# Stores ahead of the waits at stage ends, gathers in their own stage, and another order of loads and spreading units in a streaming encoder step

## The reference, cut to what matters

```python
a = rmsnorm(h, lw['norm_mix'])
z = a @ lw['w_in']                    # q, k, v, gates of both mixers
y_m, C, n, m = mlstm_chunkwise(...)   # 4 heads of 256, state C, n, m
y_f = fox_block(...)                  # 16 heads of 64, forgetting attention; sample tokens also see a cache
merge = jax.nn.sigmoid(gm) * (y_m @ lw['w_br_m']) + jax.nn.sigmoid(gf) * (y_f @ lw['w_br_f'])
h = h + merge @ lw['w_out']
h = h + peer(rmsnorm(h, lw['norm_ffn']), lw['peer_w_q'], lw['peer_keys1'], lw['peer_keys2'], lw['peer_u'], lw['peer_v'])
h = h + jax.nn.sigmoid(e @ lw['w_ple_gate']) * (p @ lw['w_ple_proj'])   # e = rmsnorm(h, lw['norm_ple'])
```

## Time and profile before

| | |
|---|---|
| median of 3 runs | 4817.5 us (4817.3 to 4831.1) |
| profiled execution | 4826.2 us, its span 4824.5 us |
| TensorE (PE) busy | 4326.6 us, 90% of the span |
| VectorE (DVE) busy | 2995.7 us, 62% |
| ScalarE (ACT) busy | 999.4 us, 21% |
| GpSimd (POOL) busy | 1260.4 us, 26% |
| bytes moved | 1477.7 MB, mean 306 GB/s |

### The profile page before, as it was taken

One profiled execution on the slowest core, in us unless ns is written; L12 is line 12 of the kernel. 1 busy time (PEld: TensorE's weight loads), 2 busy tenths in 40 slices (PEclk: granted clock), 3 DMA queues, 4 the chain that ended last, 5 costly groups with the idle time before them and its releaser, 6 DMA issues. The chain is left out here.

```text
span 4824.5 us, 49007 instructions
## 1 busy us (share of the span) xinstructions
PE 4326.6 (90%) x16974; PEld 2667.5 (55%) x16974; DVE 2995.7 (62%) x6257; ACT 999.4 (21%) x1991; POOL 1260.4 (26%) x969
## 2 busy tenths in 40 slices
PE   8997686989999996888887988869999999999988
PEld 5555453665555554666664666654545454544534
DVE  1002241458777767888870587767888777777733
ACT  1113321111001104555551122220000000000023
POOL 0000031014444442333320000004444444444400
PEclk9998788999999997878878999989999999999999
DMA  4443496769999998988958777749999999999941
GB/s 169 143 147 98 146 320 265 284 236 421 385 382 391 384 355 284 335 307 313 343 209 331 278 267 262 241 155 418 419 407 408 419 419 419 416 414 409 418 177 58
DMA packets 363496, 1477.74 MB, mean 306 GB/s; under 512 B 38338, under 2 KB 178418, under 8 KB 242706
## 3 DMA queue, kind: packets, MB, share of 16 engines
q0 software_dynamic: 119872, 824.76, 42.4%
q1 hardware_dynamic: 193874, 625.13, 34.9%
q10 hardware_dynamic: 49536, 25.17, 1.7%
HBM read 1369.00 MB, written 115.38 MB: 308 GB/s over the span
## 5 line engine op out<-in xcount | busy, mean ns | idle before, releaser
L2558 POOL DMA_INDIRECT ex_uv<-in_uv,idx x768 | 1169.6, 1523 | 1683.4 <-DVE ex_acc L2615 1487.8
L2599 DVE CUSTOM_DVE_ANT_0 ex_uv<-ex_uv,ex_xp 128x1024 f32<-128x1024 f32 x768 | 912.9, 1221 | 296.2 <-DMA ex_uv<-in_uv,idx 249.6
L2615 DVE SCALAR_TENSOR_TENSOR ex_acc<-ex_uv,ex_wt,ex_acc 128x1024 f32<-128x1024 f32 x768 | 943.0, 1281 | 10.3 <-DVE C L897 3.2
L392 PE MATMUL proj_psum_acc<-proj_w,aT_later 128*128 128x385 f32 x2304 | 748.7, 487 | 8.0 <-DMA proj_w<-in_w_in 8.0
L2813 PE MATMUL exp_psum_dn<-exp_dn_big,exp_dn_gg 128*128 128x512 f32 x1536 | 686.6, 597 | 28.3 <-DVE exp_dn_gg L2769 28.1
L2804 PE MATMUL exp_psum_dn<-exp_dn_xT,exp_dn_big 128*128 128x384 f32 x2048 | 684.3, 488 | 7.6 <-DMA exp_dn_big<-in_ud 7.6
L392 PEld LDWEIGHTS proj_psum_acc<-proj_w,aT_later 128*128 128x128 f32 x2304 | 437.0, 190 | 319.3 <-DMA proj_w<-in_w_in 8.2
L2804 PEld LDWEIGHTS exp_psum_dn<-exp_dn_xT,exp_dn_big 128*128 128x128 f32 x2048 | 390.5, 191 | 307.7 <-issue 71.2
L2813 PEld LDWEIGHTS exp_psum_dn<-exp_dn_big,exp_dn_gg 128*128 128x128 f32 x1536 | 291.8, 191 | 379.1 <-issue 351.5
L301 PE MATMUL proj_psum_acc<-proj_w,aT 128*128 128x385 f32 x1152 | 377.1, 488 | 4.2 <-DMA proj_w<-in_w_in 2.3
L301 PEld LDWEIGHTS proj_psum_acc<-proj_w,aT 128*128 128x128 f32 x1152 | 218.3, 190 | 158.9 <-issue 4.5
(11 more groups left out here) (460 smaller groups left out, 4237.1 us busy)
## 6 DMA issues: line engine op xcount, KB each, us to landing
proj_w<-in_w_in SPq DMA_DIRECT2D x48, 1540.0 KB, 7.7
rt_w<-in_w_q SPq DMA_DIRECT2D x36, 2048.0 KB, 8.7
exp_dn_big<-in_ud SPq DMA_DIRECT2D x128, 512.0 KB
exp_dn_big<-in_vd SPq DMA_DIRECT2D x128, 512.0 KB, 8.0
scratch_z<-proj_zs SPq DMA_DIRECT2D x216, 192.5 KB, 2.0
rt_w<-in_w_br_m SPq DMA_DIRECT2D x18, 2048.0 KB, 9.4
rt_w<-in_w_br_f SPq DMA_DIRECT2D x18, 2048.0 KB, 10.6
rt_w<-in_w_out SPq DMA_DIRECT2D x18, 2048.0 KB, 8.2
```

The source lines that it names most:

```text
L392: mm = pe.matmul(acc[j % SLOTS][:, 0:CW], aT[:, k, t * P:(t + 1) * P], w[:, u % U, k, :], start=(k == 0), stop=(k == KD - 1))
L2558: pool.indirect_dma_start(self.uv[:, slot, :], None, self.uv_tab, bass.IndirectOffsetOnAxis(ap=self.idx[:, at:at + 1], axis=0)).then_inc(s ...
L2599: dve.tensor_tensor_reduce(self.uv[:, slot, 0:D], self.uv[:, slot, 0:D], self.xp[:], 1.0, 0.0, ALU.mult, ALU.add, self.dot[:, g % 2, j:j + ...
L2615: dve.scalar_tensor_tensor(out=self.acc[:, j % 2, :], in0=self.uv[:, slot, D:2 * D], scalar=self.wt[:, g % 2, j:j + 1], in1=self.acc[:, j ...
```

## The change

It has five parts. (1) At the end of an attention stage SP issues the states, the last y, ncs and the last expert sum, and only then waits for landings. (2) The gathers of a hosted span begin in its own stage: `pool_ahead` fetches the first two groups of each span, and a span no longer fetches groups beyond its end. (3) The sample stage: n and m are loaded by ScalarE, the mLSTM's q, k, o, v go ahead of the states, half of the states go behind the next cache loads, and the y stores of the last two steps are issued by SP. (4) Spreading units: 28 in the steps 2 to 4 and 12 in the last, and named places for them; the third piece of the choice moves behind the next step's first four units. (5) The dense experts: the first two u blocks are loaded ahead of h, and their scores run ahead of the products that put h in place.

```diff
@@ FoxPrompt, MlstmPrompt, Gates
     def sp_last(self, sp):
-        self.sp_y(sp, H_F // 2 - 1)
         for s in range(2):
...
-    def sp_last(self, sp):
+    def sp_state(self, sp):
         NC = self.c1 - self.c0
...
+    def sp_last(self, sp):
+        if self.c1 == PT:
             sp.wait_ge(self.outs, (H_M + 2) * 16)
-        sp.wait_ge(self.y_out, NC * 16)
+        sp.wait_ge(self.y_out, (self.c1 - self.c0) * 16)
...
-    def sp_last(self, sp):
+    def sp_ncs(self, sp):
         if self.t0 == 0:
             sp.wait_ge(self.summed, 5)
...
@@ stage_attend
+            ml.sp_state(sp)
+            fx.sp_y(sp, H_F // 2 - 1)
+            ga.sp_ncs(sp)
+            if ex:
+                ex.store(sp, ex.nt - 1)
             fx.sp_last(sp)
             ml.sp_last(sp)
             ga.sp_last(sp)
             if ex:
-                ex.rows_end(sp, g1)
+                sp.wait_ge(ex.stored, ex.nt * 16)
@@ FoxSample.sp_first
         self.sp_k(sp, 0)
-        self.sp_v(sp, 0)
-        self.sp_k(sp, 1)
@@ MlstmSample
-    def sp_first(self, sp):
-        sp.dma_start(self.n_all[:].rearrange("p n h j -> p (n h j)"), self.T["n0"]).then_inc(self.state_in, 16)
+    def act_first(self, act):
+        act.dma_start(self.n_all[:].rearrange("p n h j -> p (n h j)"), self.T["n0"]).then_inc(self.state_in, 16)
...
-        for i in range(2):
-            self.sp_state(sp, i)
-        self.sp_load(sp, 0)
@@ stage_sample
             fx.sp_first(sp)
-            ml.sp_first(sp)
+            ml.sp_load(sp, 0)
+            ml.sp_state(sp, 0)
+            fx.sp_v(sp, 0)
+            fx.sp_k(sp, 1)
+            ml.sp_state(sp, 1)
...
             ml.sp_last(sp)
+            for s in range(STEPS - 2, STEPS):
+                fx.store_y(sp, s, y_last)
+            sp.wait_ge(ml.outs, 32)
+            sp.wait_ge(y_last, 2 * 8 * 16)
...
-            for s in range(STEPS):
-                fx.pool_y(pool, s)
+            for s in range(STEPS - 2):
+                fx.store_y(pool, s, fx.y_out[s % 2])
@@ Spread
-    PER_STEP = 24
+    PER_STEP = 28
+    PLACES = dict(y=(0, 4), b1=(4, 10), b3=(10, 16), x=(16, 18), q1=(18, 22), s=(22, 25), m=(25, 28))
+    LAST = dict(y=(0, 4), q1=(4, 8), s=(8, 12))
...
+    def at(self, i, place):
+        n = (i - self.FROM) * self.PER_STEP
+        full = n + self.PER_STEP <= self.UNITS
+        return self.units(i, *(self.PLACES if full else self.LAST).get(place, (0, 0)))
@@ stage_route, tensor: each spread(t, a, b) becomes place(t, name), as here
-                for u in spread(t, 10, 14):
+                for u in place(t, "b3"):
                     so.pe_spread(pe, u)
                 turn_x(t)
@@ stage_route, vector
+                    ones(t, 14, 18)
+                    if t >= 1:
+                        ch.piece(dve, chose, 7)
+                    ones(t, 18, 22)
+                else:
+                    ones(t, 4, 8)
+                    for n in (5, 6, 7):
+                        ch.piece(dve, chose, n)
+                    ones(t, 8, 12)
...
-                for u in spread(t, 18, 24):
-                    so.dve_one(dve, u)
                 if more:
+                    ones(t, 22, 28)
                     dve.wait_ge(s_out, (t + 1) * 4)
-                    for n in (0, 1, 2):
+                    for n in (0, 1):
                         ch.piece(dve, tiles[t], n)
                     if t >= Spread.FROM:
-                        for u in spread(t + 1, 0, 4):
-                            so.dve_one(dve, u)
+                        ones(t + 1, 0, 4)
+                    ch.piece(dve, tiles[t], 2)
@@ Experts
     def pool_ahead(self, pool, g0):
-        if g0 == 0:
-            for g in range(self.AHEAD):
-                self.fetch(pool, g)
+        for g in range(g0, g0 + self.AHEAD):
+            self.fetch(pool, g)
...
-            if g + self.AHEAD < self.GROUPS:
+            if g + self.AHEAD < g1:
                 self.fetch(pool, g + self.AHEAD)
@@ Dense
         sp.dma_start(self.rows_x, rows("xp")).then_inc(self.x_in, 16)
+        for c in range(AHEAD):
+            self.sp_u(sp, c, c, True)
         sp.dma_start(self.rows_h, rows("h")).then_inc(self.h_in, 16)
...
     def pe_stream(self, pe):
+        pe.wait_ge(self.turned_out, DENSE)
+        for c in range(AHEAD):
+            self.pe_score(pe, c, c, True)
         pe.wait_ge(self.h_in, 16)
...
-        for c in range(AHEAD):
-            self.pe_score(pe, c, c, True)
```

More of the change, by code:

```diff
@@ L2089, in stage_route @@
         spread = lambda i, a, b: so.units(i, a, b) if dense else ()
+        place = lambda i, name: so.at(i, name) if dense else ()
         turned = lambda i: dense and 0 <= i - Spread.FROM < DENSE
@@ L2303, in _ @@
                     turn_y(t + 1)
-                for u in spread(t, 0, 4):
+                for u in place(t, "y"):
                     so.pe_spread(pe, u)
@@ L2307, in _ @@
                     branches(t + 1, 0, 2)
-                for u in spread(t, 4, 10):
+                for u in place(t, "b1"):
                     so.pe_spread(pe, u)
@@ L2311, in _ @@
                     branches(t + 1, 2, 4)
-                for u in spread(t, 10, 14):
+                for u in place(t, "b3"):
                     so.pe_spread(pe, u)
                 turn_x(t)
-                for u in spread(t, 14, 16):
+                for u in place(t, "x"):
                     so.pe_spread(pe, u)
                 queries(t, 0, 2)
-                for u in spread(t, 16, 20):
+                for u in place(t, "q1"):
                     so.pe_spread(pe, u)
@@ L2321, in _ @@
                 scores(t)
-                for u in spread(t, 20, 22):
+                for u in place(t, "s"):
                     so.pe_spread(pe, u)
@@ L2325, in _ @@
                     turn_m(t + 1)
-                for u in spread(t, 22, 24):
+                for u in place(t, "m"):
                     so.pe_spread(pe, u)
@@ L2391, in _ @@
                     turned_y(t + 1)
-                for u in spread(t, 0, 14):
-                    so.act_clear(act, u)
+                for name in ("y", "b1", "b3"):
+                    for u in place(t, name):
+                        so.act_clear(act, u)
                 turned_x(t)
-                for u in spread(t, 14, 16):
+                for u in place(t, "x"):
                     so.act_clear(act, u)
@@ L2471, in _, with ones @@
             normed(0)
+            def ones(t, a, b):
+                for u in spread(t, a, b):
+                    so.dve_one(dve, u)
             for t in range(nt):
@@ L2474, in _ @@
                 if t == Spread.FROM:
-                    for u in spread(t, 0, 4):
-                        so.dve_one(dve, u)
+                    ones(t, 0, 4)
                 if t >= 1:
@@ L2479, in _ @@
                     ch.piece(dve, chose, 4)
[L2480 to L2483 removed]
                 if more:
+                    ones(t, 4, 6)
+                    if t >= 1:
+                        ch.piece(dve, chose, 5)
                     merge(t + 1, 0)
[L2486 to L2488 removed]
+                    ones(t, 6, 10)
                     merge(t + 1, 1)
[L2490 to L2494 removed]
+                    if t >= 1:
+                        ch.piece(dve, chose, 6)
+                    ones(t, 10, 12)
                     merge(t + 1, 2)
[L2496 to L2498 removed]
+                    ones(t, 12, 14)
                     merge(t + 1, 3)
[L2500 to L2503 removed]
+                    ones(t, 14, 18)
+                    if t >= 1:
+                        ch.piece(dve, chose, 7)
[5 more added lines that the diff above has]
+                    ones(t, 8, 12)
                 if t >= 1:
@@ L2734, in sp_stream @@
         for c in range(4):
[L2735 to L2736 removed]
+            if c >= AHEAD:
+                self.sp_u(sp, c, c, True)
+            if c == 0:
                 self.sp_block(sp, 0, 0, True)
```

43 lines of the change are left out of this document (11 added, 32 removed).

## The result

The changed kernel takes 4766.1 us as the median of three runs (4759.0 to 4767.5), where 4817.5 stood. These two medians have a ratio of 0.9893; the ratio estimated from all runs is 0.9878, with a 95% interval of 0.9861 to 0.9895. By the medians it is faster by 51 us, not by 84.5, and the median lies 2 us above the range's upper end. The profiled execution took 4767.5 us with a span of 4765.8, which is 58.7 less than the span before.

The account below looks back on a forecast made before the run. No one resource was taken to bound the kernel: each of nine stages has its own limit and ends in a barrier. Terms summed to -84.5 us, from 4817.5 to 4733 for the median; range 4708 to 4764.

Parts of the forecast that it names:

- the first attention's end: First attention stage: the store of ncs, issued right behind the last y store, goes out about 1.4 us earlier: -1.4.
- the sample's start: Sample stage: earlier m loads let TensorE begin the scores sooner, -13.3 us; mLSTM loads ahead of C save -4.4.
- the projection's end: Second projection: without the gathers of groups 52 and 53, POOL's drain no longer holds the next stage: -14.2 us.
- the second attention's end: Second attention: states before the y store and the expert sum right behind it start the next stage earlier: -12.0 us.
- the last step of the route: Route with the spreading: 12 units fewer in the DVE-bound last step, -32.5 us (bounds -26 to -36).
- the experts' start: Dense experts: u loads ahead of h gain 0 (bounds +4 and -4), since TensorE waits for the DMA anyway.
- the delay of nck: Second attention's start: eight gathers beside SP's loads delay the store of nck, +13 us (bounds +1.5 and +16.5).
- The premise on turns: Second attention's start: two busy queues take turns packet by packet, read from counts of 261 and 255 in 6 us.
- The term of +16.5: Second attention's start: upper bound for the lateness of nck, +16.5 us, if nearly all gathers go first.
- the middle steps: Route with the spreading: four more units in each of three steps, -3.6 us per step, -11 in all (bounds 0 to -15).
- 2.0 of short waits for ScalarE's clearing: Route's middle steps: an estimated 2.0 us of TensorE's waits saved per step, part of the 8.8 subtracted.
- middle steps gain nothing: Rival, 12%: in the route, DVE's units aren't hidden, so three steps lose about 4 us each: 4756 us.

Follow-up runs that it names:

- e7_sample_y_pool: The changed kernel with POOL issuing the y stores of all 16 steps of the sample stage, as before: 4769.7 us, ratio 0.9878.

## Why the prediction was right and where it was wrong

**Right, with their sizes:** the first attention's end (5.1 us from y store to next stage, now 3.8: -1.3 for -1.4; the other 2.9 us by which the stage is shorter lie in its spread, as it came out at 137 to 142 over all kernels with the change); the sample's start (-12.6 for -13.3, and -4.4) and end (from the last y product to the next stage -8.5 for -8.7, and undone it costs 10 to 11.7); the projection's end (-14.5 for -14.2); the second attention's end (-11.7 for -12.0); the last step of the route (-31.9 for -32.5); the experts' start (0).

**Wrong: the delay of nck.** The step that failed is "Bounds: +1.5 ... and +16.5 ... I take +13". The premise on turns was right: the counts are even (316 and 317), and the times of the single packets show turns of one. The inference was wrong: a turn is a packet, whatever it holds. SP's packets here are mostly rows of 0.5 KB. It moves some 8,400 packets, 5.1 MB and not the 6.2 that I worked with, in the first 21 us of the stage when it is alone, and the gathers are 1,024 rows of 8 KB. All gathers thus pass while SP gets some 64 of its small rows on each DMA engine, and nck came 22.7 us later, which is the whole transfer of the gathers and a little more. The term of +16.5 that I called an upper bound was too low, and the rows behind the choice stood beside loads of 4 KB pieces. The rule of the Trainium skill, page "DMA: Bandwidth & Descriptors", section "Queues, rings and completion order", by which several descriptors are drained before the switch, gave +16.5 for this term, nearer; but the times of the single packets in both traces show turns of one, so it was nearer by another cause. That the gathers are the cause of the 22 us is shown by the kernel that takes them back; that they need not be is shown by the one that starts them at 21.0 us.

The other 7.5 us by which this stage's last y store was late are not the change's, as far as the runs show: the same stage code gave bodies of 595.9 to 610.5 us in seven kernels with the gathers at the start, and the three with later gathers gave 587.1, 598.2 and 604.5. What goes with it is the granted clock over the body, from 0.84 (583.1 us) over 0.81 (593.6 before, 595.9 to 597.0 in four kernels) to 0.77 (610.5): TensorE is busy for 489 to 529 us in it, VectorE for 514 to 515 in all of them. Why the clock is granted differently isn't settled, and a few us of the difference could still be the gathers'.

**Wrong: the middle steps.** "4.0 + 1.2 - 8.8 = -3.6 per step" failed in its first and its last term. The 6.8 us of waits for one-hots went in the last two steps, as it says, and of 12.5 in the first, which the forecast took as 6.8, 6.2 stayed. But the four units cost 5.5 us a step and not 4.0 (346.9 and 330.5 us for three steps that differ by 12 units and by no wait for x), and the "2.0 of short waits for ScalarE's clearing" did not go: a wait for x took their place, because the 16th unit now stands ahead of x and with it ScalarE's issue of a store. ScalarE's clearing itself held TensorE for 9.0 us over the three steps before and 8.0 after. I had counted ScalarE's copies and not the DMA that every fourth one issues. Together the three steps are 2.7 us shorter than before as a mean of eight kernels and 3.4 longer in the one profile of the changed kernel; forecast were 11. The rival "middle steps gain nothing" is thus what came, by another mechanism than it named: DVE was not the bound.

**The range.** The two misses have one sign, 9.7 us for nck and 8 to 14 for the middle steps, and the body's clock moves the whole by more than 10 us between executions. I had left no room for the latter, though the three runs before lay 14 us apart.

## What to carry to other kernels

Where two queues feed the same DMA engines, compare what one packet of each holds. A burst of large rows passes nearly whole ahead of a queue of small ones, so where a small store on the critical path is near, hold the burst until the loads that the store depends on have landed, or start it early enough to be over. POOL pays a drain at the barrier that grows with the DMAs it issued in the stage; have its last issues done well before the end, and give those that fall at the end to an engine without such a drain, here SP (7 ns). When pieces of work are moved past a hand-over on an engine, count what that engine issues for them, not only what it computes.

## What the runs showed of the hardware

POOL's drain at a barrier goes with the number of DMAs that POOL issued in the stage. In the sample stage it was 10507 ns after 128 stores (before, and in `e7_sample_y_pool`) and 9201 ns after 112 (the changed kernel and nine others, to the nanosecond), so 82 ns for each. In the routes it was 548 ns after 6 DMAs and 1046 after 13, behind some 170 gathers 12.8 to 14.1 us and behind some 210 of them 16.7 to 18.1, that is 76 to 91 ns for each. It doesn't get shorter when the others still have work: in the changed kernel 17443 ns ran from 1738.0, right behind POOL's last gather and 34 us ahead of the next stage. The experts' stage is an exception, 958 ns after 393 DMAs, and why is open. SP's drain at the ends of the sample, projection and attention stages took 7 ns.

The granted clock fell to 0.5 (1.2 GHz) behind idle stretches of 2 to 5 us of TensorE in the route's steps, and not each time, as some stretches of 2.2 and of 4.5 us were followed by no fall. Middle steps with the same instructions took from 116.6 to 121.3 us, with granted clocks of 0.99 to 0.93. In the kernel without the wait for x they took 115.4 to 115.8.
